# Index keys, index weights and time steps as one 48-column chunk with the weights held still, and values computed with channels on partitions and then transposed

## The reference

```python
(u_pool, q, kv, qi, ki, wi, u_conv, z, xbc, dt_raw, gate_logits) = jnp.split(h @ w_in, offsets, axis=-1)
k, v = jnp.split(kv, 2, axis=-1)
ki = rope_partial(ki.reshape(bsz, seq, 1, IDX_DIM), IDX_ROPE_DIM)[:, :, 0, :]
y_b = dsa_attention(q, k, v, qi, ki, wi)
y_c = conformer_conv(u_conv, conv_dw, conv_b, conv_ln_g, conv_ln_b)
y_d = mamba2_mixer(z, xbc, dt_raw, ...)
```

## Time and profile before

| what | value |
|---|---|
| median of 3 runs | 1969.56 us (1968.22 to 1969.62) |
| profiled execution, own time | 1960.89 us |
| its span, first to last instruction | 1959.1 us |
| mean granted TensorE clock | 0.967 of full |
| TensorE busy | 1842.4 us, 94% of the span |
| VectorE busy | 1521.7 us, 78% |
| ScalarE busy | 1131.3 us, 58% |
| input projection of layer 0, gt copied out to g2h0 started | 45.97 to 139.84 us |
| the same in layer 1 | 594.61 to 694.74 us |

### The profile page before, as it was taken

The page is one execution under the profiler, slowest core; times in us unless marked ns, Lnnn a source line. Parts: engine busy times, 40 slices in busy tenths (PEclk is TensorE's granted clock), DMA queues, the critical chain, the costliest instruction groups (busy, mean ns, idle before and its releaser), DMA issues.

```text
span 1959.1 us, 28204 instructions
## 1 busy us (share of the span) xinstructions
PE 1842.4 (94%) x10776; PEld 1622.6 (83%) x10776; DVE 1521.7 (78%) x1487; ACT 1131.3 (58%) x925; POOL 5.1 (0%) x13
## 2 busy tenths in 40 slices
PE   6999889899989998897899999999999999999996
PEld 6989878799979988786788888888888888888884
DVE  3979957545448789766788989889898898988985
ACT  3335554443433265544577767777677776777764
POOL 0000000000000000000000000000000000000000
PEclk9999999999988899999899999999999999999997
DMA  6435334665334334345599999999999999999991
GB/s 231 147 113 165 119 105 132 231 206 181 127 112 152 119 130 148 111 132 202 177 381 337 360 357 364 356 349 361 367 352 358 348 359 379 342 361 342 358 377 66
DMA packets 232259, 485.50 MB, mean 248 GB/s; under 512 B 16992, under 2 KB 41568, under 8 KB 232048
## 3 DMA queue, kind: packets, MB, share of 16 engines
q1 hardware_dynamic: 231120, 479.65, 69.2%
q0 software_dynamic: 1056, 4.70, 0.6%
HBM read 483.24 MB, written 1.05 MB: 247 GB/s over the span
## 4 chain that ended last, share of the span: by engine, by line
PE 81%; DVE 12%; ACT 4%; issue 1%; DMA 1%; SPq 0%; DVEq 0%; ACTq 0%
PE pair L815 56%; PE aux L815 19%; DVE lo_ring L1308 3%; PE aux L1199 2%; PE pair L1221 1%; ACT hi_ring L432 1%; PE aux L1272 1%; DMA raw_ring<-in_w_in 1%; DVE arena L1540 1%; DVE arena L1489 1%; DVE arena L1475 1%; DVE small L1488 1%; DVE pair L1465 0%; DVE arena L1554 0%; ACT arena L477 0%
## 5 line engine op out<-in xcount | busy, mean ns | idle before, releaser
L1308 DVE TENSOR_TENSOR lo_ring<-raw_ring,hi_ring 128x2048 fp32r<-128x2048 f32 (+2 forms) x278 | 623.3, 2246 | 146.1 <-ACT hi_ring L432 144.2
L432 ACT ACTIVATE hi_ring<-raw_ring 128x2048 fp32r<-128x2048 f32 (+2 forms) x278 | 522.5, 1881 | 304.3 <-PE pair L815 221.9
L1308 DVE TENSOR_TENSOR lo_ring<-arena,hi_ring 128x2048 fp32r<-128x2048 f32 x183 | 417.6, 2289 | 99.0 <-ACT hi_ring L432 97.4
L432 ACT ACTIVATE hi_ring<-arena 128x2048 fp32r<-128x2048 f32 x183 | 350.3, 1918 | 152.6 <-PE aux L815 81.4
L815 PE MATMUL pair<-hT_lo,hi_ring 128*128 128x256 f32 x1328 | 389.5, 293 | 22.7 <-DVE lo_ring L1308 7.9
L815 PE MATMUL pair<-lo_ring,hT_hi 128*128 128x512 f32 (+3 forms) x992 | 382.3, 385 | 3.9 <-DVE hT_lo L1813 2.4
L815 PE MATMUL pair<-hT_hi,lo_ring 128*128 128x256 f32 x1328 | 383.7, 289 | 0.0
L815 PE MATMUL pair<-hT_hi,hi_ring 128*128 128x256 f32 x1328 | 383.2, 289 | 0.0
L815 PE MATMUL pair<-hi_ring,hT_hi 128*128 128x512 f32 (+3 forms) x992 | 377.9, 381 | 0.0
L815 PE MATMUL pair<-hi_ring,hT_lo 128*128 128x512 f32 (+3 forms) x992 | 377.4, 380 | 0.0
L815 PEld LDWEIGHTS pair<-hT_lo,hi_ring 128*128 128x128 f32 x1328 | 262.8, 198 | 30.4 <-ACT arena L477 9.7
(11 more groups left out here) (278 smaller groups left out, 1886.8 us busy)
## 6 DMA issues: line engine op xcount, KB each, us to landing
raw_ring<-in_mu SPq DMA_DIRECT2D x222, 512.0 KB, 5.7
arena<-in_mg SPq DMA_DIRECT2D x220, 512.0 KB, 5.2
raw_ring<-in_w_in SPq DMA_DIRECT2D x120, 512.0 KB, 4.5
arena<-in_md SPq DMA_DIRECT2D x114, 512.0 KB, 5.4
raw_ring<-in_md SPq DMA_DIRECT2D x110, 512.0 KB, 5.4
raw_ring<-in_w_br SPq DMA_DIRECT2D x32, 512.0 KB, 4.5
raw_ring<-in_w_out SPq DMA_DIRECT2D x16, 512.0 KB, 4.3
raw_ring<-in_fg SPq DMA_DIRECT2D x12, 512.0 KB, 4.0
```

The lines of the kernel that those rows point to most:

```text
L432: nc.scalar.activation(hi_ring[:, h, 0:cols], raw(slot)[:, 0:cols], ACT.Copy).then_inc(hi_ready, 1)
L1308: nc.vector.tensor_tensor(lo_ring[:, h, 0:cols], raw(slot)[:, 0:cols], hi_ring[:, h, 0:cols].bitcast(f32), ALU.subtract).then_inc(lo_ready, 1)
```

## The change

The chunk kiwi becomes kwdt: 48 columns, the 32 of `ki`, the 8 of `wi` and the 8 of `dt_raw`, computed with the 48 weight columns as the stationary operand and the 256 tokens moved past them (24 matmuls per layer in place of 48). The values become an ordinary `t_block` of kvqi (24 matmuls in place of 48). The 8 columns fall away from xbc1 (48 matmuls fewer). Both new results have channels on the partitions, so after pool TensorE repeats the keys to 128 partitions by a matmul with a new constant `rep4`, and transposes the 48-row chunk and the values, two token blocks each. ScalarE copies index weights, time steps, values and keys out of that, in four instructions before `ki_copied`. The panels of kwdt are loaded by one DMA of 40 columns and one of 8 each. TensorE's wait for the constants comes ahead of the transposes, and VectorE's first step on the time steps waits for `ki_copied` in place of xbc1.

```diff
+                        sp.dma_start(v[:, :, 0:40], rows[:, :, C_KIWI:C_KIWI + 40]).then_inc(raw_in[slot], 16)
+                        sp.dma_start(v[:, :, 40:KWDT], rows[:, :, C_DT:C_DT + 8]).then_inc(raw_in[slot], 16)
...
-                after("kiwi")
-                g = pair_of("kiwi")
-                for b in range(NB):
-                    evac(ar3(A_KI + b * 128, 4, 32), g[:, b * 40:b * 40 + 32].unsqueeze(1).broadcast_to([128, 4, 32]))
-                    evac(ar(A_MISC + b * 8, 8), g[:, b * 40 + 32:b * 40 + 40], last=(b == NB - 1))
+                after("kwdt")
+                evac(arena[0:KWDT, A_KI:A_KI + T], pair_of("kwdt")[0:KWDT, 0:T], last=True)
...
                 act.wait_ge(S["ki_turned"], L + 1)
+                turned = aux[:, 512:640].rearrange("p (b c) -> p b c", b=2)
+                nc.scalar.activation(ar3(A_MISC, 2, 8), turned[:, :, 32:40], ACT.Copy)
+                nc.scalar.activation(ar3(A_MISC + 16, 2, 8), turned[:, :, 40:48], ACT.Copy)
+                nc.scalar.activation(ar(A_V, 256), aux[:, 1024:1280], ACT.Copy)
                 nc.scalar.activation(ar(A_IDX + 512, 256), aux[:, 0:256], ACT.Copy).then_inc(S["ki_copied"], 1)
...
-                        if name == "xbc1":
-                            for b in range(NB):
-                                ins = n_block(g[:, 512 + b * 8:520 + b * 8], w, 256, 8, b, kh, kh == 0 and b == 0)
...
-                        for b in range(NB):
-                            ins = n_block(pair_of("kiwi")[:, b * 40:(b + 1) * 40], w, 0, 40, b, kh, kh == 0 and b == 0)
+                        for k in range(4):
+                            ins = split_mm(pair_of("kwdt")[0:KWDT, 0:T], (w[0][:, k, :], w[1][:, k, :]),
+                                           (hT_hi[:, 4 * kh + k, :], hT_lo[:, 4 * kh + k, :]), kh == 0 and k == 0,
+                                           kh == 1 and k == 3)
...
-                            n_block(g[:, 256 + b * 128:384 + b * 128], w, 128, 128, b, kh, False)
...
+                t_chunk("kvqi")
...
+                pe.matmul(aux[:, 0:256], consts[0:32, CONSTS["rep4"][0]:CONSTS["rep4"][0] + 128], arena[0:32, A_KI:A_KI + T],
+                          start=True, stop=True)
                 for b in range(NB):
-                    ins = pe.transpose(aux[:, b * 128:(b + 1) * 128], ar(A_KI + b * 128, 128), C("ident"))
+                    pe.transpose(aux[:, 512 + b * 64:512 + b * 64 + KWDT], arena[0:KWDT, A_KI + b * 128:A_KI + (b + 1) * 128],
+                                 consts[0:KWDT, CONSTS["ident"][0]:CONSTS["ident"][0] + KWDT])
+                for b in range(NB):
+                    ins = pe.transpose(aux[:, 1024 + b * 128:1024 + (b + 1) * 128], ar(A_KI + T + b * 128, 128), C("ident"))
...
-                t_chunk("xbc1", 2, 264)
+                t_chunk("xbc1", 2, 256)
...
-                dve.wait_ge(*ev(L, "xbc1"))
+                dve.wait_ge(S["ki_copied"], L + 1)
```

More of the change, by code:

```diff
@@ L58 @@
 C_POOL, C_Q, C_KVQI, C_KIWI = 0, 512, 1024, 1536
-C_A, C_GT, C_Z, C_XBC0, C_XBC1, C_GATE = 1576, 2088, 2600, 3112, 3624, 3888
-CHUNKS = [("a", 2, "A"), ("gt", 2, "A"), ("kiwi", 2, "A"), ("kvqi", 2, "A"), ("q", 2, "A"), ("pool", 2, "A"),
+C_A, C_GT, C_Z, C_XBC0, C_XBC1, C_DT, C_GATE = 1576, 2088, 2600, 3112, 3624, 3880, 3888
+KWDT = 48
+CHUNKS = [("a", 2, "A"), ("gt", 2, "A"), ("kwdt", 2, "A"), ("kvqi", 2, "A"), ("q", 2, "A"), ("pool", 2, "A"),
           ("xbc0", 2, "A"), ("xbc1", 2, "A"), ("lnsum", 0, "D"), ("z", 2, "A"), ("lnvar", 0, "D"),
@@ L85 @@
                ("swap", 128), ("cosq", 256), ("sinq", 256), ("cosi", 256), ("sini", 256), ("iota", 128),
-               ("invcnt", 64), ("far", 256), ("causal", 128), ("rev8", 8), ("iota8", 8)):
+               ("invcnt", 64), ("far", 256), ("causal", 128), ("rev8", 8), ("iota8", 8), ("rep4", 128)):
     CONSTS[_n] = (_c, _w)
@@ L272, in chunk_in, with narrow @@
                         panel(width, w_in[L, kh * 512:(kh + 1) * 512, c0:c0 + width].rearrange("(k p) n -> p k n", p=128))
-                for c0, width in ((C_A, 512), (C_GT, 512), (C_KIWI, 40), (C_KVQI, 512), (C_Q, 512), (C_POOL, 512),
-                                  (C_XBC0, 512), (C_XBC1, 264), (C_Z, 512)):
-                    chunk_in(c0, width)
+                def narrow():
+                    nonlocal i
+                    for kh in range(2):
+                        slot, _ = MSLOT[L][i]
+                        if slot in last:
+                            sp.wait_ge(lo_ready, last[slot] + 1)
+                        v = raw(slot)[:, 0:4 * KWDT].rearrange("p (k n) -> p k n", n=KWDT)
+                        rows = w_in[L, kh * 512:(kh + 1) * 512, :].rearrange("(k p) n -> p k n", p=128)
+                        sp.dma_start(v[:, :, 0:40], rows[:, :, C_KIWI:C_KIWI + 40]).then_inc(raw_in[slot], 16)
+                        sp.dma_start(v[:, :, 40:KWDT], rows[:, :, C_DT:C_DT + 8]).then_inc(raw_in[slot], 16)
+                        last[slot] = MIX_BASE[L] + i
+                        i += 1
+                for c0, width in ((C_A, 512), (C_GT, 512), (C_KIWI, KWDT), (C_KVQI, 512), (C_Q, 512), (C_POOL, 512),
+                                  (C_XBC0, 512), (C_XBC1, 256), (C_Z, 512)):
+                    if c0 == C_KIWI:
+                        narrow()
+                    else:
+                        chunk_in(c0, width)
                 def gates(n):
@@ L502, in mixer @@
                 evac(ar(A_QK + 1024, 256), g[:, 0:256])
-                evac(ar(A_V, 256), g[:, 256:512])
+                evac(ar(A_KI + T, T), g[:, 256:512])
                 evac(ar(A_IDX, 512), g[:, 512:1024], last=True)
@@ L514, in mixer @@
                 g = pair_of("xbc1")
-                evac(ar3(A_XBCP, 6, SPAD + T)[:, 4:6, SPAD:], g[:, 0:512].rearrange("p (g t) -> p g t", t=T))
-                evac(ar(A_MISC + 16, 16), g[:, 512:528], last=True)
+                evac(ar3(A_XBCP, 6, SPAD + T)[:, 4:6, SPAD:], g[:, 0:512].rearrange("p (g t) -> p g t", t=T), last=True)
                 def gate(name, before=None):
@@ L852, in t_block @@
                     return ins
[L854 to L858, removed]
                 def t_panel(name, kh, groups=4, width=512):
@@ L881, in mixer @@
                 t_chunk("gt")
-                free("kiwi")
+                free("kwdt")
                 for kh in range(2):
                     def body(w):
-                        for b in range(NB):
-                            ins = n_block(pair_of("kiwi")[:, b * 40:(b + 1) * 40], w, 0, 40, b, kh, kh == 0 and b == 0)
-                        return ins
[L888 to L894, removed]
-                            n_block(g[:, 256 + b * 128:384 + b * 128], w, 128, 128, b, kh, False)
-                        t_block(g[:, 512:768], w, 256, kh, kh == 0)
-                        return t_block(g[:, 768:1024], w, 384, kh, False)
-                    panel(512, body)
+                        for k in range(4):
+                            ins = split_mm(pair_of("kwdt")[0:KWDT, 0:T], (w[0][:, k, :], w[1][:, k, :]),
+                                           (hT_hi[:, 4 * kh + k, :], hT_lo[:, 4 * kh + k, :]), kh == 0 and k == 0,
+                                           kh == 1 and k == 3)
+                        return ins
+                    panel(KWDT, body)
@@ L899, in mixer @@
+                t_chunk("kvqi")
                 t_chunk("q")
                 t_chunk("pool")
-                pe.wait_ge(*ev(L, "kiwi"))
+                if L == 0:
+                    pe.wait_ge(const_in, 16)
+                pe.wait_ge(*ev(L, "kvqi"))
                 pe.wait_ge(S["hT_lo_done"], 4 * (2 * L + 1))
+                pe.matmul(aux[:, 0:256], consts[0:32, CONSTS["rep4"][0]:CONSTS["rep4"][0] + 128], arena[0:32, A_KI:A_KI + T],
+                          start=True, stop=True)
                 for b in range(NB):
-                    ins = pe.transpose(aux[:, b * 128:(b + 1) * 128], ar(A_KI + b * 128, 128), C("ident"))
+                    pe.transpose(aux[:, 512 + b * 64:512 + b * 64 + KWDT], arena[0:KWDT, A_KI + b * 128:A_KI + (b + 1) * 128],
+                                 consts[0:KWDT, CONSTS["ident"][0]:CONSTS["ident"][0] + KWDT])
@@ L906, in mixer @@
+                for b in range(NB):
+                    ins = pe.transpose(aux[:, 1024 + b * 128:1024 + (b + 1) * 128], ar(A_KI + T + b * 128, 128), C("ident"))
                 ins.then_inc(S["ki_turned"], 1)
                 t_chunk("xbc0")
-                if L == 0:
-                    pe.wait_ge(const_in, 16)
                 pe.wait_ge(S["ki_copied"], L + 1)
@@ L1895, in mixer_cols @@
 def mixer_cols():
-    width = {"kiwi": 40, "xbc1": 264}
+    width = {"kwdt": KWDT, "xbc1": 256}
     return [4 * width.get(n, 512) for n, k, _ in CHUNKS for _ in range(k)]
@@ L1918, in constants @@
     put("iota8", np.arange(8)[None, :])
+    put("rep4", i[:, None] == i[None, :] % 32)
```

## The result

The changed kernel takes 1944.89 us (median of 4 runs, 1944.21 to 1947.3), the kernel before 1968.95 us beside it (4 runs, 1968.22 to 1969.62): ratio 0.9894, 95% interval 0.9869 to 0.9919. By the medians that is 24.1 us faster where 16.2 were forecast; the recorded ratio stands for 20.9 us. Later runs of before have medians of 1966.16, 1964.78 and 1965.44 us, and where both kernels ran beside each other again (after_again) the medians differ by 21.7 us, so some 21 us is the better figure. Between the profiled executions the gain is 1960.89 - 1944.21 = 16.7 us. It is smaller because the profiled execution of before was a quick one for its kernel; the first experiment takes this up.

What follows compares the result with a forecast made beforehand. TensorE and VectorE were taken to run neck and neck, VectorE's waits and lead capping the gain: 5.6 + 11.8 - 1.0 - 0.15 = 16.2 us off the 1969.6 us median, giving 1953.4 us, range 1946.5 to 1961.5.

Steps and rivals of the forecast that it cites:

- VectorE bounds the gain: Convolution up to lnsum: the gain can be no more than VectorE's waits and lead, whatever TensorE is spared.
- S: Span from start of gt copy-out to start of lnsum, forecast at about 75.8 us in both layers.
- The saving of kiwi goes into a wait: Before kvqi: kiwi's 2.4 us per layer doesn't reach the end; TensorE waits some 5.2 us instead of 2.79.
- 48 stationary columns: In kwdt: a matmul with 48 stationary columns costs 0.12 us, so 24 take 2.9 us.
- Layer 0, 5.6 us, layer 1, 11.8 us: lnsum starts earlier, right behind the convolution's last tap: by 5.6 us in layer 0, 11.8 us in layer 1.
- 1.0 us lost at lnsum: After TensorE's new wait for the last tap, half clock costs lnsum 0.5 us per layer, 1.0 in all.
- Copies hidden: Three more ScalarE copies ahead of ki_copied, 0.6 to 1.1 us, still leave panel 14's high part in time.
- rival 4: Slower: the new 8-column DMA lands late, delaying the convolution; needs 26 us per landing; 1978 us, chance 0.02.
- Constants, 0.15 us: At the start: 64 KB more constants, loaded by the first panels' engines, cost 0.15 us.
- rival 2: Layer 1's bad stretch is untypical, both layers give only 5.6 us: 1959.6 us, chance 0.17; the other way round, 1947.
- Rival 1: kvqi stays at half clock because of longer idleness before it: 5.0 us lost in both, 1955.9 to 1958.4 us, chance 0.17.
- Rival 3: No change, since VectorE's lead is given back after lnsum: 1966 to 1973 us, chance 0.04.

Runs made afterwards that it cites:

- after_again: The changed kernel, unchanged, run once more beside the kernel before: 1943.7 us, ratio 0.9891.
- the first experiment: The kernel before, unchanged, with more runs to read their spans and granted clock: 1968.83 us, ratio 1.0015.
- keys_only: The kernel before with only the 40-column chunk of index keys and weights transposed: 1965.02 us, ratio 0.9998.
- wide_fill: The changed kernel plus 40 unused matmuls of 256 moved columns in TensorE's wait before kvqi: 1945.87 us, ratio 0.9897.
- before_again: The kernel before, unchanged, with more runs: 1968.83 us, ratio 1.0015.
- before_fewer_taps: The kernel before with the last 4 of the convolution's 31 taps left out: 1967.75 us, ratio 1.0017.
- before_reordered: The kernel before with z moved ahead of the LayerNorm sums, g2h0's first half ahead of the variance, panel parts made earlier: 1964.63 us, ratio 0.9998.
- narrow_fill: The changed kernel plus 40 unused matmuls of 40 moved columns in TensorE's wait before kvqi: 1943.68 us, ratio 0.9893.
- values_only: The kernel before with only the values turned into a t_block of kvqi: 1951.38 us, ratio 0.9933.

## Why the prediction was right, and where its sizes were off

- **The time.** 1944.89 us is 8.5 us below the 1953.4 forecast and 1.6 below the low end of 1946.5. Put on the median that the forecast started from, the ratio gives 0.9894 x 1969.56 = 1948.7 us, inside the range and 4.7 us below the forecast. So the direction and the mechanism were right and the gain was taken too small.
- **VectorE bounds the gain.** Right. S was forecast as 75.8 us in both layers and is 75.67 and 75.68. Fewer taps help only the changed kernel, and keys_only wins nothing.
- **The saving of kiwi goes into a wait** of "some 5.2 us". Measured 5.31.
- **48 stationary columns** at 0.12 us. Measured 0.115 from start to start; nothing hung on it.
- **Layer 0, 5.6 us, layer 1, 11.8 us.** S fell by 5.8 and 12.0 between the two first profiles. The rest between them is small: gt 0.4 us later, 0.9 back between the layers, 1.4 lost behind the start of layer 1's g2h0, which now begins at a clock of 0.67. That the sum of 16.2 comes so near to the 16.7 between the profiles is in part luck: it had 1.0 us lost at lnsum that was not lost, and nothing for this 1.4.
- **1.0 us lost at lnsum.** Not seen: it ran at 1.00 in both layers, after waits of 2.1 and 1.8 us. wide_fill shows the loss where the wait is 4.17 us, 1.8 us a layer. The upper bound of 1.7 a layer was near, the value taken was too high for waits of 2 us.
- **Copies hidden.** The four took 92.55 to 93.22 us, 0.67 in all, and panel 14 was not late. The small DMAs landed in 2.5 us, far from the 26 that rival 4 needs:

```profile
consts<-in_consts POOLq DMA_DIRECT2D x1, 1256.0 KB, 13.4
raw_ring<-in_w_in SPq DMA_DIRECT2D x4, 80.0 KB, 2.1
...
raw_ring<-in_w_in SPq DMA_DIRECT2D x4, 16.0 KB, 2.5
```

- **Constants, 0.15 us.** They land in 13.4 us in place of 13.0. What that costs can't be seen: the gt copy-out of layer 0 begins anywhere from 45.85 to 47.23 us in four profiles of kernels with before's projection.

- **The mis-sized term is layer 0's gain, as counted against the median.** The sum used layer 0 as profiled, 4.5 us of half clock, and took 16.2 us from a median 8.7 us above that execution, without asking what those 8.7 us were. Of four profiled executions in which kiwi, the values and the time steps are as in before (before, before_again, before_fewer_taps, before_reordered), three have 17 us of half clock in layer 0, so there layer 0 wins 11.0 us, not 5.6. The prediction had this as the other side of rival 2, "6 us more are won: 1947"; with the 1.0 us at lnsum it makes 1946.4, against 1944.9 by the median and 1948.7 by the ratio. Rival 2 itself, layer 1 as quick as the profiled layer 0, is seen in none of the four (17.0 to 17.1 us in three of them, 10.3 in one); the two quickest of 30 runs, 1953.5 and 1953.8 us at a clock of 0.971 and 0.972, would fit it, but they were not profiled.
- **Rival 1**, half clock calls for idleness and stays, fell: kvqi had 4.8 and 5.4 us of it after 5.3 us of idleness, at 0.80 and 0.78 over 12.1 us where the rival had 0.50. The Trainium skill ("TensorE: Matmul & The Clock Gate", part 1) has idleness as what throttles the clock again; that it does so is seen here, in kvqi. But the runs show a second cause beside it, the narrow matmuls: in layer 1 of narrow_fill the clock falls within them and without idleness.
- **Rival 3** fell: lnsum to g2h0 takes 12.51 us now, 12.43 before.
- **Two slips of addition.** The high end is 1959.6 + 2.4 = 1962.0, not 1961.5, and the chances that make it faster are 0.60 + 0.17 + 0.17 = 0.94, not 0.93. Nothing hung on either.

Still open: what sets whether layer 0 of before loses 4.5 or 17 us in a given run. The mean clock tells the two apart, but not why.

## What to carry to other kernels

When two engines run neck and neck, work taken from the busier one wins only the other's lead and waits; read the first instruction that needs both, and measure its distance from their common start. Before a sum from one profile is taken from a median, explain the gap between the two: here it was, most likely, a stretch at half clock that this one execution had escaped. After the change, the order written for the old bound is worth another look: moves that won nothing before it won 7 us after it.

## What was unexpected in the hardware

TensorE's clock fell to 1.2 GHz in the middle of back-to-back matmuls of 40 moved columns. TensorE in order of time, before_again, layer 0:

```profile
51.08 0.27 PE L815 MATMUL pair<-hi_ring,hT_lo 128*128 128x40 f32 x1
51.19 0.38 PE L815 MATMUL pair<-hi_ring,hT_hi 128*128 128x40 f32 x1
51.40 0.38 PE L815 MATMUL pair<-lo_ring,hT_hi 128*128 128x40 f32 x1
```

The distance of starts goes from 0.11 to 0.21 us at 51.19, with no idleness ahead of it, and the half clock lasts until 68.19. The same fall within kiwi is seen in 11 of the 12 layers profiled with a kiwi of 40 or 48 moved columns; the twelfth is layer 0 of the first profile of before. These stretches at half clock were 17 us long with narrow kiwi and narrow values, 12.9 and 11.7 with narrow values alone (keys_only, after 5.3 us of idleness), 10 with narrow kiwi alone (values_only), about 5 with neither but the idleness, none with wide matmuls in place of it. They do not follow the forms alone: with narrow kiwi and narrow values that same layer 0 had 4.5 us, after 2.79 us of idleness, and layer 1 of before_reordered 10.3. A narrow matmul took nearly as much time as a wide one (0.11 against 0.12 us), and the wide ones behind it took 0.21 us each until the half clock ended.
